# Two transformer blocks on one core: one tile of weight sums to each pair of columns, moved casts, loads and sums around the two feed-forward parts

## What is computed

```python
# first block: gated feed-forward, then a gated embedding
h = rms_norm(x, norm_ffn)
x = x + (silu(h @ w_ffn_gate) * (h @ w_ffn_up)) @ w_ffn_down      # 1024 -> 2816 -> 1024
gate = sigmoid(rms_norm(x, norm_ple) @ w_ple_gate)
x = x + gate * (p @ w_ple_proj)
# second block: a causal convolution of 3 taps between the two maps
u = causal_dwconv(h @ w_up, conv_w, conv_b)                       # 1024 -> 5632 = gate | value
y = (gelu(u[:, :2816]) * u[:, 2816:]) @ w_down
x = x + g2 * rms_norm_2(y, post_ffn_g)
```

## Time and profile before

| | before |
|---|---|
| runs | 2734.04, 2734.07 and 2738.77 us, median 2734.07 us |
| the profiled execution's own time | 2730.18 us |
| its span, first to last instruction | 2728.4 us |
| PE busy | 2594.0 us, 95% of the span |
| DVE, ACT, POOL busy | 1812.1, 1179.6 and 1184.5 us |
| mean granted PE clock | 0.987 of full |

### The profile page before, as it was taken

One profiled execution on the slowest core, in us unless ns is written; L12 is line 12 of the kernel. 1 busy time (PEld: TensorE's weight loads), 2 busy tenths in 40 slices (PEclk: granted clock), 3 DMA queues, 4 the chain that ended last, 5 costly groups with the idle time before them and its releaser, 6 DMA issues.

```text
span 2728.4 us, 32147 instructions
## 1 busy us (share of the span) xinstructions
PE 2594.0 (95%) x11826; PEld 2084.9 (76%) x11826; DVE 1812.1 (66%) x2180; ACT 1179.6 (43%) x2084; POOL 1184.5 (43%) x767
## 2 busy tenths in 40 slices
PE   7999999999899999999999999998999999999997
PEld 6887788888687877888877778877767777777785
DVE  6888866653977777688834546427378666666686
ACT  6777421122533333344544333356354444444444
POOL 2454522233455555555633211134433544555457
PEclk9999999999899999999999999999999999999999
DMA  3000044432355554465522112122321122125664
GB/s 122 24 24 24 20 156 153 152 105 106 110 183 201 201 198 177 172 207 184 174 70 86 57 33 46 38 74 70 131 85 62 70 84 78 70 79 176 233 194 144
DMA packets 125916, 311.96 MB, mean 114 GB/s; under 512 B 13368, under 2 KB 26936, under 8 KB 122816
## 3 DMA queue, kind: packets, MB, share of 16 engines
q1 hardware_dynamic: 125760, 309.91, 33.8%
HBM read 248.45 MB, written 61.41 MB: 114 GB/s over the span
## 4 chain that ended last, share of the span: by engine, by line
PE 50%; DVE 22%; DMA 9%; POOL 7%; ACT 6%; issue 5%; SPq 0%; POOLq 0%; ACTq 0%; DVEq 0%
PE psum_mem L768 20%; PE psum_mem L1093 8%; POOL w_lo L3991 4%; PE psum_mem L1063 4%; DMA w_raw<-in_w_up_b 3%; DVE tmp_mem L3696 3%; DMA w_raw<-in_w_ffn_up 3%; PE psum_mem L1262 2%; DVE tmp_mem L3039 2%; PE psum_mem L1267 2%; PE psum_mem L1264 2%; PE psum_mem L830 2%; DVE w_raw L2958 2%; DMA x_ring_b<-hidden 1%; ACT w_hi L1852 1%
## 5 line engine op out<-in xcount | busy, mean ns | idle before, releaser
L3991 POOL TENSOR_TENSOR w_lo<-w_raw,w_hi 128x512 fp32r<-128x512 f32 x364 | 553.2, 1525 | 555.5 <-ACT w_hi L1852 476.0
L3897 POOL TENSOR_TENSOR w_lo<-w_raw,w_hi 128x1024 fp32r<-128x1024 f32 (+2 forms) x105 | 236.5, 2252 | 626.4 <-ACT w_hi L1617 543.9
L1852 ACT CAST w_hi<-w_raw 128x512 fp32r<-128x512 f32 x364 | 223.3, 619 | 436.5 <-PE psum_mem L1093 169.7
L1063 PE MATMUL psum_mem<-h_hi,w_hi 128*128 128x512 f32 x672 | 270.9, 403 | 28.2 <-ACT parts L1917 19.9
L1063 PE MATMUL psum_mem<-h_hi,w_lo 128*128 128x512 f32 x672 | 267.3, 398 | 14.1 <-POOL w_lo L3991 14.1
L1063 PE MATMUL psum_mem<-h_lo,w_hi 128*128 128x512 f32 x672 | 265.6, 395 | 0.0
L768 PE MATMUL psum_mem<-h_hi,w_hi 128*128 128x512 f32 x736 | 232.6, 397 | 11.8 <-ACT h_hi L1651 9.3
L768 PE MATMUL psum_mem<-h_lo,w_hi 128*128 128x512 f32 x736 | 229.1, 393 | 5.7 <-DVE h_lo L3606 5.5
L768 PE MATMUL psum_mem<-h_hi,w_lo 128*128 128x512 f32 x736 | 228.3, 392 | 2.7 <-POOL w_lo L3897 2.7
L1617 ACT CAST w_hi<-w_raw 128x1024 fp32r<-128x1024 f32 (+2 forms) x105 | 100.1, 954 | 268.5 <-PE psum_mem L768 255.9
L1063 PEld LDWEIGHTS psum_mem<-h_hi,w_hi 128*128 128x128 f32 x672 | 128.4, 191 | 72.0 <-ACT parts L1917 28.1
(11 more groups left out here) (465 smaller groups left out, 6357.9 us busy)
## 6 DMA issues: line engine op xcount, KB each, us to landing
hidden<-tmp_mem SPq DMA_DIRECT2D x44, 512.0 KB, 2.9
down_sums<-sum_raw SPq DMA_DIRECT2D x22, 1024.0 KB, 6.7
w_raw<-down_sums SPq DMA_DIRECT2D x88, 256.0 KB, 3.8
w_raw<-in_w_up_b SPq DMA_DIRECT2D x44, 512.0 KB, 4.7
x_ring_a<-hidden SPq DMA_DIRECT2D x66, 256.0 KB, 3.8
x_ring_b<-hidden SPq DMA_DIRECT2D x66, 256.0 KB, 3.7
w_raw<-in_w_in_a SPq DMA_DIRECT2D x32, 512.0 KB, 3.7
ada_raw<-in_w_ada SPq DMA_DIRECT2D x64, 256.0 KB, 3.3
```

The lines of the kernel that those rows point to most:

```text
L1063: made = e.matmul(out, wt, x, start=j <= DIFF_3 and k == 0 and part == 0, stop=k == KH - 1 and part == 2, skip_group_check=True)
L1852: e.copy(w_slot(w_hi, slot, of), source).then_inc(*S.of("w_hi", key))
L3897: e.tensor_tensor(w_lo[:, i, 0:width], w_raw[:, i, 0:width], w_hi[:, i, 0:width].bitcast(F32), ALU.subtract).then_inc(*S.of("w_lo", c))
L3991: e.tensor_tensor(w_slot(w_lo, slot, of), source, w_slot(w_hi, slot, of).bitcast(F32), ALU.subtract).then_inc(*S.of("w_lo", key))
```

## The change

It has these parts:

1. `sum_tiles_beside` gives one tile to each of pairs 1 to 21; the 22nd tile is made in the first down map (loaded behind unit 5's weights, summed by DVE at unit 13, stored behind unit 19's weights).
2. All four sums of a tile stand behind `b_sum` and `weight_high_sum` on DVE (`tile_sums`).
3. `keep_x_a` moves to the place of `form_hi` in SBUF, so the first down map's buffers no longer lie on `sum_raw`. SP no longer waits for the last two tiles of sums ahead of it. The place of `p_hi`, `p_lo` and `p_raw` is now free only late, and the loads of `p`, its cast and its low part move from units 11, 15 and 18 to units 70, 72 and 74.
4. In both down maps the weights of units 0 and 1 are loaded ahead of the first four kept hidden tiles.
5. At the end of the first down map ACT and POOL take the next stage's first weight tile (`ahead(1)`) ahead of the last rows of squares instead of behind them.
6. In the second block's pairs ACT makes the gelu of a pair in the next pair, behind its UP_HIGH cast, and so behind the cast of SUM_1 and the copy of UP_LOW too; SP stores `hidden` behind the two loads of weights of each pair.
7. In the second down map the eight loads of `x_last` (512 KB each) go out one each four units, from unit 33 on, instead of all at unit 33.
8. There the sum of squares of the first half goes from unit 70 to 72, and what follows it one unit later each: ACT's inverse and copy from units 74 and 75 to 75 and 76, DVE's part from 75 to 76.

```diff
 def sum_tiles_beside(i):
 
-    return [n for n in range(len(SUM_TILES)) if 1 + n * 19 // len(SUM_TILES) == i]
+    return [i - 1] if 0 < i < KF else []
...
+        with ExitStack() as downs:
+            keep_x_a = sb_in(downs, "keep_x_a", [P, KB, HALF])
         form_hi_mem = sb_in(ff1, "form_hi", [P, 3, KH, HALF], F32R)
         with ExitStack() as downs:
             x_ring_a = sb_in(downs, "x_ring_a", [P, 4, HALF])
-            keep_x_a = sb_in(downs, "keep_x_a", [P, KB, HALF])
...
             def first_half_sum(u):
-                if u == 6 * KB + 4:
+                if u == 6 * KB + 6:
                     end_sum(0)
...
-                if u == 15:
+                if u == 6 * KB + 6:
                     for k in range(2):
                         w.wait_ge(f"in_p{k}", 0)
                         e.copy(p_hi[:, k, :], p_raw[:, k, :]).then_inc(*S.of("p_hi", k))
...
+            ahead(1)
             for k in range(KH):
                 ple_row(k, 1)
-            ahead(1)
...
                 fill_pair(i, UP_HIGH, "b")
+                if i > PLAIN:
+                    gelu(i - 1)
                 fill_pair(i, GATE_HIGH, "b")
...
                 tap_first(i, 1, up_banks(i))
-                if i == KF - 1:
-                    down_unit("b", 3)
-                gelu(i)
                 if i < KF - 1:
                     fill_pair(i + 1, SUM_1, "b")
+                else:
+                    down_unit("b", 3)
+                    gelu(i)
...
             for _, i in FFN_PAIRS:
-                for n in sum_tiles_beside(i):
-                    first_tile_sums(n)
                 if i >= 2:
                     w.wait_ge(f"hid_out{i % 2}", ("a", i - 2))
                 b_sum(i)
...
                 weight_high_sum(i)
                 for n in sum_tiles_beside(i):
-                    last_tile_sums(n)
+                    tile_sums(n)
...
-                if u == 15:
+                if u == KB + 2:
+                    tile_sums(len(SUM_TILES) - 1)
+                elif u == KB + 4:
                     gains()
-                elif u == 18:
+                if u == 6 * KB + 8:
                     for k in range(2):
                         w.wait_ge("p_hi", k)
...
-            for n in (20, 21):
-                w.wait_ge(f"ws_out{n % 2}", n)
+            w_load("a", 0)
+            w_load("a", 1)
             kept_loads("a", 0)
-            for u in range(4):
-                w_load("a", u)
+            w_load("a", 2)
+            w_load("a", 3)
...
+                if u == 5:
+                    sum_out(len(SUM_TILES) - 2)
+                    sum_load(len(SUM_TILES) - 1)
+                elif u == KB + 8:
+                    sum_out(len(SUM_TILES) - 1)
...
-                if u == KB:
+                if u == 6 * KB + 4:
+                    w.wait_ge("dn_xl", ("a", 6 * KB - 1))
                     for k in range(2):
                         e.dma_start(p_raw[:, k, :], io["p"][k]).then_inc(*S.of(f"in_p{k}", 0, 16))
...
             for i in range(PLAIN, KF):
-                if i >= 4:
-                    hidden_out("b", i - 2)
                 for row in (1, 0) if i > PLAIN else (0, 1):
                     back_emptied(i, row)
                     name, c = raw_event("b", ("pair", i), row)
                     e.dma_start(w_raw[:, c % 2, 0:unit_width[c]], units[c][1]).then_inc(*S.of(name, c, 16))
-                if i < 4:
-                    hidden_out("b", i - 2)
+                hidden_out("b", i - 2)
             hidden_out("b", KF - 2)
...
-                if u == 3 * KB:
-                    for k in range(KD):
+                if u >= 3 * KB and (u - 3 * KB) % 4 == 0 and u < 3 * KB + 4 * KD:
+                    for k in ((u - 3 * KB) // 4,):
                         e.dma_start(x_last[:, k, :], io["x_park"][k]).then_inc(*S.of(f"in_l{k}", "last", 16))
```

More of the change, by code:

```diff
@@ L2606, in scalar @@
                         logarithms()
-                elif p == 6 and kt == 8:
+                elif p == 6 and kt == 9:
                     end_inverse(0)
-                elif p == 6 and kt == 9:
+                elif p == 6 and kt == 10:
                     end_norm(0)
@@ L3081, in down_add, with tile_sums @@
                     *S.of("x1", ("dn", p, mi, TARGETS[m][t])))
-            def first_tile_sums(n):
+            def tile_sums(n):
                 low, high, late, high_late = (sum_part(n, j) for j in range(4))
@@ L3088, in first_tile_sums @@
                 e.tensor_tensor(high, low, high, ALU.subtract).then_inc(*S.of("ws_sum", (n, M_7)))
-            def last_tile_sums(n):
-                low, high, late, high_late = (sum_part(n, j) for j in range(4))
                 w.own("ws_sum")
@@ L3172, in vector @@
                                         ALU.subtract).then_inc(*S.of("p_lo", k))
-                elif p == 3 and kt in (1, 3, 5, 7):
+                if p == 3 and kt in (1, 3, 5, 7):
                     ple_low(kt // 2, 0)
@@ L3873, in vector @@
                     back_add(p, mi)
-                if u == 6 * KB + 9:
+                if u == 6 * KB + 10:
                     end_inverse(0)
@@ L4589, in sync @@
                     e.dma_start(w_raw[:, c % 2, 0:unit_width[c]], units[c][1]).then_inc(*S.of(name, c, 16))
-                if i < 4:
-                    hidden_out("b", i - 2)
+                hidden_out("b", i - 2)
             hidden_out("b", KF - 2)
+            w_load("b", 0)
+            w_load("b", 1)
             kept_loads("b", 0)
-            for u in range(4):
-                w_load("b", u)
+            w_load("b", 2)
+            w_load("b", 3)
             for part in (1, 2):
```

## The result

| | before | changed |
|---|---|---|
| runs | 2732.53 to 2738.77 us (4), median 2734.06 | 2655.30 to 2658.96 us (4), median 2657.04 |
| ratio | 1 | 0.9714, 95% interval 0.9699 to 0.9730 |
| profiled execution, and its span | 2730.18, 2728.4 us | 2658.96, 2657.1 us |
| PE busy | 2594.0 us, 95% | 2566.2 us, 97% |
| mean granted PE clock | 0.987 | 0.992 |

The changed kernel is 77 us faster, 2.9%. 67.7 were forecast. By the ratio the result is 2655.9 us, which is 10 us under the forecast of 2666 and 1.1 under the range's lower end of 2657. Measured again (e9), the same kernel took 2658.35 us (0.9728, 0.9714 to 0.9741).

A forecast was written before the change was run, and what follows sets the result against it. PE, busy 95% of the span, was taken as the bound. Six terms summed to 67.7 us off the profiled 2730.18 us, giving 2662.5; 3.9 added for the median gave 2666 us, range 2657 to 2690.

The forecast's parts named there:

- B: Second block's pairs: gelu a pair later, weights ahead of the hidden store, PE becomes the bound; 26.5 us back (17 to 29).
- Rival 1: Second block: the loop, not PE, stays the bound at a period of 19.8 us; 12 us less gain, 2678; chance 0.15.
- rival 2: First block: GATE_HIGH waits for DVE's gate read behind the four sums; 15 us less gain, 2681; chance 0.10.
- rival 3: First block: loads hold its period, so it gains less than forecast; 9 us do not come back, 2675; chance 0.06.
- A: First block's pairs: one tile of sums each, behind the bank's add, removes waits for ACT's copy; 25.7 us back (10.7 to 26.7).
- C: Second down map: spread x_last loads give back 6.9 us (5.7 to 6.9), weights ahead of kept tiles 3.2 (0 to 5.4).
- D: End of first down map and p: earlier weight cast removes PE's wait, moved p work costs some; 6.5 us back (4.0 to 7.5).
- E: Program's end: later sum of squares saves 1.2 us, later outputs and adds lose 2.3; -1.1 us (+1.4 to -2.4).

The follow-up runs named there:

- e9: Changed kernel once more, unedited, as the measure for the others and as a second trace of it; 2658.35 us, ratio 0.9728.
- e1: Changed kernel with the first two sums of each tile ahead of the bank's add again, one tile to a pair kept; 2676.64 us, ratio 0.9792.
- e8: Changed kernel with six DVE instructions per tile in place of four, two extra maximums ahead of the fourth sum; 2670.03 us, ratio 0.9776.
- e2: Changed kernel with the gelu of the second block's pairs back in its own pair, hidden store still behind the loads; 2681.16 us, ratio 0.9811.
- e4: Changed kernel with the eight loads of x_last in one go at unit 33 again; 2666.06 us, ratio 0.9755.
- e11: Changed kernel with the first four kept hidden tiles loaded ahead of the weights of units 0 and 1 again, both down maps; 2659.75 us, ratio 0.9734.
- e7: Changed kernel with the next stage's first weight cast (ACT) and low part (POOL) behind the last rows of squares again; 2664.20 us, ratio 0.9759.
- e12: Changed kernel with unit 2's low part between the last pair's taps and the second half's last adds behind two outputs, not four; 2657.04 us, ratio 0.9721.
- e6: Changed kernel with the first half's sum of squares back at unit 70 and ACT's and DVE's following work as before the change; 2655.78 us, ratio 0.9727.
- e3: Changed kernel with each hidden store of the second block's pairs ahead of the two weight loads again, gelu still a pair later; 2658.79 us, ratio 0.9729.
- e5: Changed kernel with the first half's sum of squares left at unit 72, but ACT's and DVE's following work as before the change; 2659.10 us, ratio 0.9737.

## Why the prediction was wrong: the right mechanism, and one term too small

The step that failed is the size of B. The forecast gave 26.5 us to the second block's pairs, with 29 as the most; 31.1 and 32.0 us came back. The forecast's lower end was the sum of the upper ends, B's 29 among them, and so the result fell 1.1 us below it.

**What bounds, and which waits go: right.** PE was the bound, every wait named was there, and every one that was to go is gone. None of the four rivals decided. Rival 1 (the loop stays the bound) fell by the period, 375.15 / 1644 = 0.2282 us a matmul; rival 2 (GATE_HIGH) by the slack of 1.1 us, read twice, and it came in pair 1 alone, for 0.65 us; rival 3 (the loads hold the first block) by 1704 matmuls without a wait at a higher DMA rate than before, 197 GB/s against 194.

**A: right, its parts too.** 25.7 forecast; 27.8 and 25.3 in the two pairs of traces. Pair 1 is 1.0 us longer than the others, as forecast. The row's price for a slow sum was right, and so was two slow and two fast. On this the Trainium skill ("SBUF — State Buffer", section "Who interferes with whom") has the rule by which a sum waits for the one POOL instruction that it meets. The traces agree: 1.66 us for each of two sums beside three low parts in a row (e1), 0.69 for both of the extra ones in e8, where POOL has nothing to do.

**B: too small, the step that failed.** 26.5 forecast, 31.1 and 32.0 measured. The mechanism was right, and so were its rows: the load takes 4.62 us without the store ahead of it (e2; 4.65 estimated), and the high sum fell to 0.80 (0.69). Two numbers of the sum were not right. First the price of a matmul: I read 0.228 from 216 matmuls in 49.25 us. Into that piece fall the slower first matmuls behind a wait and the modelled end of the last matmul; the next stage's first matmul starts at 1154.74, and 49.09 us less 0.1 for those first matmuls is 0.2268 each. The error of 0.0012 us is 0.5%, but it is taken from 1596 matmuls, 1.9 us of B, and 1.8 of A. Secondly, "what remains lost" was put at 4.7 us: 2.2 for the first pairs and 2.5 for slow loads. Measured: 375.15 - 1644 x 0.2268 = 2.3 in all, and it lies in the first two pairs (21.24 and 19.19 us against 19.04). So the 2.2 was right, and the 2.5 should have been 0. DVE waits for the loads by 1.4 to 3.3 us in all pairs but one, and nothing of it reaches PE: in most pairs DVE still has some idle time ahead of the bank's add, 0.99 us in the pair shown. The stated best case of 29 therefore lay under what was possible: all that the stretch lost before is, by the right price, 406.23 - 372.9 = 33.4 us.

**C: right in sum, in part for the wrong reason.** 11.3 forecast with the sum of squares, 11.4 and 11.5 measured. e4 gives 7.3 to 7.7 for the loads of x_last (6.9 forecast). The 3.2 for the weights ahead of the kept tiles were given to the wrong part: e11 shows that this order brings little or nothing, and e2 that the entry's wait hangs on the gelu. And part of what was won there went to a wait that I had not looked for, at unit 2, for a low part behind DVE's taps. It was there before and is twice as long now:

```profile
2493.70 0.50 PE L1093 MATMUL psum_mem<-x_lo_b,w_hi 128*128 128x512 f32 x1 [1.45 <-DVE x_lo_b L3066]
```

```profile
2427.50 0.50 PE L1094 MATMUL psum_mem<-x_lo_b,w_hi 128*128 128x512 f32 x1 [2.90 <-DVE x_lo_b L3069]
```

From the entry's wait to the end of this one PE took 12.1 us before and takes 9.7 now: 2.4 us back of the 3.2. That the sum came out right is luck in part.

**D: right for the wait.** 6.5 forecast, 6.7 and 11.4 measured. `x_lo` at unit 75 is late by 1.31 us, as forecast (1.3). The 11.4 come from the second trace of the kernel before, which was slower there; e7 gives 8.7 by its trace for the cast, and 5 to 8 by the times.

**E: right in sign; in size by one trace.** -1.1 forecast; with the sum's wait of 1.23 us it is -2.7 and -1.0. What was missed is that PE waits 1.95 us at the end for the last square. What follows differs from trace to trace: behind that wait the last eight matmuls take 5.4 us at a lower clock in the first trace and 3.7 in the second, and that is the whole difference of 1.7 between the two.

**The frame.** 2730.18 us was taken as the kernel's time and 3.9 added to come to its median. The median of the changed kernel isn't 3.9 above its profiled execution; it is 1.9 below it. A profiled execution is one draw. With the difference of the medians in place of the frame, the terms of the first pair of traces, 71.3, still miss 5.7 of the 77; the second pair, 78.4, passes it by 1.4. So by the first pair, of the 9.3 us by which the forecast was too high, 3.6 are the terms (B's 4.6, the others together -1.0), and 5.7 are the draw; by the second pair all of it is terms, B's 5.5 and D's 4.9 first. B is the one term that lies above its own upper bound in both (A's 27.8 does so in the first alone, D's 11.4 in the second), and with 31 to 32 in place of 29 the lower end of the range would have been 2654 to 2655.

What stays open: how much of A, D and the middle is the change's and how much the draw's, to 2 or 3 us each. Part 3 (the place of `keep_x_a` and of `p`) was not undone by itself, nor was the distribution of the tiles; its 7 to 10 us are a difference and not a run. Why the clock fell behind a wait in some traces and not in others is open too.

## What to carry to other kernels

Where PE is the bound, take the price of a matmul from a stretch without any wait, from one instruction's start to another's start, and with the count of matmuls worked out from the program; half a percent of error in it is the size of a term when it is multiplied by thousands. Here a loop over several engines gave back all of its loss once its period dropped under PE's: ask for the period it would have, and if that is lower, take the whole loss as the upper end, less what the first rounds lose, and price delays at zero as long as they fit in the slack. And an instruction that is moved is only safe if the engine has idle time behind it: the four sums had 6.0 us of room and took 4.85; behind the low part of e12 DVE had none, and the wait came back at the next units.

## What the runs showed of the hardware

The same wait doesn't always bring the same clock. At unit 2 of the second down map PE waits 2.84 us in e6 and 2.90 in the changed kernel, for the same instruction, behind the same units. The windows of e6, then of the changed kernel, over the same 7 us behind it:

```profile
2427.00:2434.00 7.00, 6.59 (x17) 5.22 (x18) 6.90 (x8) 2.97 (x6) 4.44 (x3) 0.55 0.22 76
```

```profile
2427.00:2434.00 7.00, 6.32 (x26) 4.91 (x27) 6.90 (x8) 3.07 (x6) 4.26 (x3) 1.00 0.06 24
```

In one the granted clock goes to 0.55, near the lower level of 1.2 GHz, and 17 matmuls run; in the other it stays at 1.00 and 26 run. Ten traces have a wait of 2.8 to 3.0 us at this instruction: in six the clock stays at 1.00 behind it (e4, e5, e7, e8 and both of the changed kernel), in four it falls (e1, e3, e6, e11). The wait of 1.95 us at the end of the program is in nine traces, and behind it the clock falls in three (changed kernel, e3, e4) and stays in six.

All fourteen traces, twelve of the experiments and one of each kernel, took 689.4 to 694.3 us for the stages between the two feed-forward parts, which no edit touches. Single waits differ there too; one for ACT's `k_tok` is between 0.9 and 2.8 us long. Runs of one kernel lie up to 6 us apart, likely for the same reason, which was not shown, since only one run of each kernel was traced. So edits worth 2 us, as part 8 or e12, can be read in a trace but not in a time.
